# Hyena on one Trainium2 core: the gates issued behind the first of four sums instead of behind all four

## What is computed

```python
def hyena_mixer(x, w_in, w_short, ..., d_bias, w_o):
    u = dwconv_centred(x @ w_in, w_short)
    v, g1, g2 = jnp.split(u, 3, axis=-1)
    z = v
    for o, gate in enumerate((g1, g2)):
        k_f = jnp.fft.rfft(two_sided_kernel(filt[:, o, 0], filt[:, o, 1]), n=n, axis=0)
        z_f = jnp.fft.rfft(z, n=n, axis=1)
        y = jnp.fft.irfft(z_f * k_f, n=n, axis=1)[:, :length]
        z = gate * (y + d_bias[o] * z)
    return z @ w_o
```

## Time and profile before

| | us |
|---|---|
| median of 3 runs | 1926.57 |
| lowest, highest | 1926.17, 1926.86 |
| profiled execution | 1927.07 |
| its span | 1925.8 |
| TensorE matmuls busy | 1793.5 |
| DVE busy | 997.6 |
| GpSimd busy | 782.1 |
| ACT busy | 629.9 |

### The profile page before, as it was taken

One profiled execution on the slowest core, in us unless ns is written; L12 is line 12 of the kernel. 1 busy time (PEld: TensorE's weight loads), 2 busy tenths in 40 slices (PEclk: granted clock), 3 DMA queues, 4 the chain that ended last, 5 costly groups with the idle time before them and its releaser, 6 DMA issues.

```text
span 1925.8 us, 19804 instructions
## 1 busy us (share of the span) xinstructions
PE 1793.5 (93%) x7880; PEld 1435.0 (75%) x7880; DVE 997.6 (52%) x1371; ACT 629.9 (33%) x889; POOL 782.1 (41%) x360
## 2 busy tenths in 40 slices
PE   3588799999999899999999999998998999999997
PEld 1455688888877676678888888777887778888785
DVE  7786533332135567475444413589897564444124
ACT  1332322222124445244333312442232243333222
POOL 3533244444443302134444444356563434444442
PEclk9797899999999899999999999999998999999998
DMA  8673223333222201022322332522222223223322
GB/s 308 231 273 120 79 97 99 99 98 97 91 98 70 79 12 55 27 83 88 97 92 96 99 98 88 185 89 98 77 81 84 88 76 95 94 97 99 98 88 77
DMA packets 54342, 197.45 MB, mean 103 GB/s; under 512 B 6216, under 2 KB 6664, under 8 KB 52393
## 3 DMA queue, kind: packets, MB, share of 16 engines
q1 hardware_dynamic: 52584, 190.05, 29.6%
q10 hardware_dynamic: 1666, 6.14, 0.9%
HBM read 183.58 MB, written 12.58 MB: 102 GB/s over the span
## 4 chain that ended last, share of the span: by engine, by line
PE 77%; DVE 14%; ACT 3%; POOL 2%; issue 2%; DMA 2%; SPq 0%; ACTq 0%; DVEq 0%
PE ps L482 25%; PE ps L484 24%; PE ps L483 24%; DVE x_residual L2090 1%; POOL w_lo L1488 1%; DVE act_lo L1800 1%; DVE n_values L1795 1%; PE ps L872 1%; PE ps L527 1%; ACT act_hi L1173 1%; DVE mod_ring L1665 1%; PE ps L596 1%; DVE x_residual L2081 1%; DMA n_values<-in_hy_fw_out 1%; DVE x_residual L1778 1%
## 5 line engine op out<-in xcount | busy, mean ns | idle before, releaser
L1488 POOL TENSOR_TENSOR w_lo<-w_raw,w_hi 128x1024 fp32r<-128x1024 f32 x250 | 608.9, 2437 | 914.2 <-ACT w_hi L1064 914.2
L482 PE MATMUL ps<-act_hi,w_hi 128*128 128x512 f32 x1364 | 541.1, 397 | 29.2 <-POOL w_lo L1488 13.2
L483 PE MATMUL ps<-act_lo,w_hi 128*128 128x512 f32 x1364 | 534.9, 392 | 0.0
L484 PE MATMUL ps<-act_hi,w_lo 128*128 128x512 f32 x1364 | 534.7, 392 | 0.0
L1064 ACT ACTIVATE w_hi<-w_raw 128x1024 fp32r<-128x1024 f32 x250 | 264.8, 1060 | 785.6 <-PE ps L484 780.8
L482 PEld LDWEIGHTS ps<-act_hi,w_hi 128*128 128x128 f32 x1364 | 258.2, 189 | 94.8 <-issue 15.6
L484 PEld LDWEIGHTS ps<-act_hi,w_lo 128*128 128x128 f32 x1364 | 258.3, 189 | 54.9
L483 PEld LDWEIGHTS ps<-act_lo,w_hi 128*128 128x128 f32 x1364 | 258.5, 190 | 53.0 <-issue 1.0
L482 PE MATMUL ps<-f_hidden_hi,w_hi 128*128 128x512 f32 x528 | 208.3, 394 | 1.9 <-POOL w_lo L1488 1.9
L484 PE MATMUL ps<-f_hidden_hi,w_lo 128*128 128x512 f32 x528 | 206.9, 392 | 0.0
L483 PE MATMUL ps<-f_hidden_lo,w_hi 128*128 128x512 f32 x528 | 206.2, 391 | 0.0
(11 more groups left out here) (268 smaller groups left out, 2433.9 us busy)
## 6 DMA issues: line engine op xcount, KB each, us to landing
w_raw<-in_w_stream SPq DMA_DIRECT2D x258, 512.0 KB, 3.6
mod_ring<-in_mod_t SPq DMA_DIRECT2D x26, 512.0 KB, 5.6
x_tokens<-in_mod_t SPq DMA_DIRECT2D x22, 512.0 KB, 5.9
spectra<-filter_spectra SPq DMA_DIRECT2D x16, 512.0 KB, 3.4
hy_filter<-spectra SPq DMA_DIRECT2D x8, 1024.0 KB, 4.8
x_residual<-in_xT ACTq DMA_DIRECT2D x8, 256.0 KB, 7.3
x_tokens<-in_x_tokens SPq DMA_DIRECT2D x1, 2048.0 KB, 8.0
x_spill<-x_residual SPq DMA_DIRECT2D x8, 256.0 KB, 2.9
```

The costliest lines, as they stand in the source:

```text
L482: PE.matmul(o, lh, rh, start=start, stop=False, **kw)
L483: PE.matmul(o, lh, rl, start=False, stop=False, **kw)
L484: return PE.matmul(o, ll, rh, start=False, stop=stop, **kw)
L1488: GP.tensor_tensor(low, B.WR[:, c % 2, :], f32(high), ALU.subtract).then_inc(S.w_lo, 1)
```

## The change

At two places of DVE's list the four sums are issued in two parts, the first sum alone and then the other three, and the four gates stand between them instead of behind. `sums` gets two arguments for that. No instruction is added or left out, and each keeps its waits. The lists of the other engines are as they were.

```diff
-        def sums(half, f):
+        def sums(half, f, low=0, high=4):
             s = 2 * half + f
             VE.wait_ge(S.filter_read, s + 1)
             for dst, x1, x2, op, v in ((1, 4, 6, ALU.add, S.v_cos), (5, 4, 6, ALU.subtract, S.v_cos),
-                                       (3, 0, 2, ALU.add, S.v_sin), (7, 0, 2, ALU.subtract, S.v_sin)):
+                                       (3, 0, 2, ALU.add, S.v_sin), (7, 0, 2, ALU.subtract, S.v_sin))[low:high]:
                 VE.wait_ge(v, s + 1)
                 VE.tensor_tensor(X[:, dst, :], X[:, x1, :], X[:, x2, :], op).then_inc(S.prod, 1)
...
         branches(12, 13)
-        sums(1, 0)
+        sums(1, 0, 0, 1)
         gates(0)
+        sums(1, 0, 1, 4)
         prod_lo(1, 0)
...
         plus_sin()
-        sums(3, 0)
+        sums(3, 0, 0, 1)
         gates(2)
+        sums(3, 0, 1, 4)
         prod_lo(3, 0)
```

## The result

| | before | changed |
|---|---|---|
| median, 6 executions each | 1926.37 | 1914.21 |
| lowest, highest | 1922.35, 1927.17 | 1911.59, 1917.54 |
| profiled execution | 1927.07 | 1911.67 |
| its span | 1925.8 | 1910.4 |

The ratio is 0.9945, with a 95% interval of 0.9931 to 0.9958, so about 10.6 us less (8.1 to 13.3); the two medians alone stand 12.2 us apart. A second set of executions of the same two kernels gave 0.9958 (0.9942 to 0.9974), 8.1 us less.

What follows compares the result with a forecast made beforehand. TensorE, busy 93% of the span, was taken as the bound, idling for gates queued behind sums on DVE. Gains of 1.8 + 4.0 + 1.7 = 7.5 us took the median from 1926.57 to 1919.1, range 1916.0 to 1922.3.

Steps and rivals of the forecast that it cites:

- The pauses: TensorE's idle times at A and B, waiting for the gates: from 4.24 to 2.4 us and 5.33 to 1.35 us.
- R3: Rival at B: the gates are held by `w_lo` like the second sum; 3.5 us gained, 1923.1 us, chance 0.05.
- The tap's row: Convolution tap, one PSUM and one SBUF operand, 0.74 us inside `w_lo`; by it a gate costs its 0.674 us.
- the sum's row: Second sum at B, 2.86 us beside `w_lo`; by it gates would be held and B gain 1.7 instead of 4.0.
- DVE's room: DVE's spare time ahead of the next butterflies after A and B: 1.4 us each, so TensorE's gain passes on whole.
- R4: Rival: the path isn't shortened, another wait meets the gain; at most 0.2% left, about 1924.5 us, chance 0.05.
- R5: Rival, slower: DVE waits for `S.back` at B's fourth gate with its queue behind; 1931 us, chance 0.03.
- The clock: TensorE's granted clock, halved after both pauses: slow shares 2.1 us at A, 1.7 at B; 1.7 booked at B only.
- B: Place ahead of `forward(3, 1)` where TensorE idles 5.33 us for the gates; start forecast 4.0 us earlier, full clock 1.7 more.
- A: Place ahead of `forward(1, 1)` where TensorE idles 4.24 us for the gates; start forecast 1.8 us earlier.
- R1: Rival: the clock stays high at A too, 2.1 us more gained, 1917.0 us, chance 0.14.
- R2: Rival: clock falls in B's short pause or the shifted 2.67 us one; 1920.8 us, both 1922.5, chance 0.11.

Runs made afterwards that it cites:

- waiting split: Kernel before, order of sums and gates kept, but at B GpSimd starts `w_lo` only when the four sums are done; ratio 0.9984 (0.9965 to 1.0002).
- B alone: Kernel before with the change made only at B, A left as before; ratio 0.9971 (0.9960 to 0.9983).

## Why the prediction was right, and where it was wrong

- **The pauses.** Right, both to 0.05 us. The step that carries them, first gate to first matmul 2.62 us, held, and so did the places taken by the first gate.
- **Gates beside GpSimd.** Right: 2.47 us for four inside the split. R3 falls. The tap's row was the right one, and the unchanged order with a waiting split shows that the sum's row measured the hold. The Trainium skill (SBUF — State Buffer, "Who interferes with whom") has a DVE instruction with two SBUF inputs contend with a GpSimd instruction that reads SBUF, and one with at most one such input not; both measurements agree with it, the four gates of 2.47 us and the four sums of 3.47 instead of 5.65.
- **DVE's room.** Right: 1.34 and 1.36 against 1.4 us. R4 falls, and R5 doesn't decide even with 6 to 7 us of waiting.
- **The clock.** B stayed high as booked. At A the forecast booked nothing: it stayed high (+2.1 by that working), and the moved 2.67 us pause fell instead (1.4 to 1.7 off). R1 and R2 were given as alternatives, and both came, with terms that nearly cancel: that was luck. At A the same pause lost the clock in another execution. The 2.67 us pause kept the clock only in the two profiles of the kernel before. It lost it in eleven others (in the twelfth it is 4.82 us long), with B alone and with the waiting split too, where A is as before; so one profile's kept clock had been taken for the rule, and a chance of 0.11 for R2 was too small. The shares were read from one profile and treated as prices; the runs show 3.4 to 6.1 us of half clock behind B's first matmul alone.
- **The sum.** 7.5 us; the stretch says 8.0 and 7.3 us, against the first and the second profile of the kernel before, and the second set of executions 8.1 (5.0 to 11.2). The forecast of the change itself was right by these. The first set's interval, 8.1 to 13.3 us, leaves it just outside.
- **What failed is the base and its spread**, the step from the 7.5 us to a median of 1919.1 and its range. The prediction took the three executions shown, 1926.17 to 1926.86, as the kernel's spread, and gave a range made of the mechanism's cases alone; a term for what the rest of the program does from execution to execution wasn't in it. The measured median is 12.4 us below the base of 1926.57, and the stretch accounts for 8.0 of them. An unchanged kernel takes 1917 to 1936 us, with medians of 1922.7 to 1925.5 in the later sets. Of the 15.4 us between the first two profiles nearly half, 7.0, lay ahead of A: 2.8 between the pause near 800 us and A, where one of the two has the fall of the clock, and 4.2 before that pause, which begins between 794 and 803 us in the fourteen profiles. The clock goes with this earlier part as well. Ahead of that pause TensorE had about 61 us of half clock in the five profiles that reach it earliest (794.5 to 797.9) and 75 to 78 us in four of the six that reach it last (800.9 to 802.7). Some of that half clock lies in pauses, so it isn't shown to be the cause, and what moves the earlier part stays open. The range had to be wider by some 3 us on each side, the faster and the slower one, an estimate from the 3.7 us that the unchanged kernel's own medians span (1922.7 to 1926.4).

## What to carry to other kernels

Where an engine on the critical path waits for a result, put in its producer's list only what must stand ahead of it; an instruction with slack that can be held by another engine costs its worst time there, not its own. When such a hold is to be removed, follow the held resource to the next instructions of the same kind, for the hold moves on to them. And before a few tenths of a per cent are forecast from one profile, take a second profile of the unchanged kernel, look for pauses in which the clock fell in one and not in the other, and count them into the range. Time a stretch around the change, not only the whole.

## What the chip showed that I had not expected

- Pauses of one length at one instruction keep the clock or lose it from execution to execution: 2.43 to 2.44 us at A kept it in three profiles and lost it in one; 2.86 to 2.88 us near 800 us lost it in six and kept it in eight; 2.67 us in the Hyena stage kept it in two and lost it in eleven.
- Moving one GpSimd instruction of 2.8 us out of the way of a DVE instruction made it 2.4 us long and the DVE one 0.68 instead of 2.86 us, so both are faster apart.
- The three instructions of `plus_sin` at A take 0.68 us each with GpSimd idle and 1.7 to 2.9 beside it, so the 7 us of waiting that the gates ahead of `plus_sin` brought there gave back 4 (from the first of them to the instruction behind the third it is 1.9 us, and 6.2 in the changed kernel).
